# One transformer step with product-key experts: V rows gathered per token, one tile behind the u rows

## The chip, the cores and the metric

The kernel runs as one program on one core of a Trainium2 chip. The metric is the device time of one execution in microseconds (us); lower is better. Everything is float32.

## The reference

A layer computes adaLN modulation, an input projection, stick-breaking attention and a pooled branch, an output projection with residual, and then the part that matters here, PEER:

```
q  = h2 @ w_query                       # 8 heads, two halves of 128
s1, s2 = q[:,0] @ keys1, q[:,1] @ keys2 # 128 scores a half
v1,i1 = top16(s1); v2,i2 = top16(s2)
cand = v1[:,None] + v2[None,:]          # 256 sums
best, sel = top16(cand); idx = i1*128+i2 at sel
gate = softmax(best)
act  = gelu(h2 . u_tab[idx])            # one dot product an expert
out  = sum((gate*act) * v_tab[idx])     # 8*16 = 128 experts a token
x    = x + gate2 * RMSNorm(out)
```

There are 1024 prompt tokens (8 tiles of 128) and 64 sample tokens (one tile, called tile 0). `u_tab` and `v_tab` have 16,384 rows of 1024 floats (4 KB a row), so each token needs 128 rows of each.

## The kernel before, in words

`build` runs five stages one after the other: `modulation`, `projection`, `attention`, `output`, `experts`. The first four are left as they are but for the search of the sample tile, which runs inside `output` between its tiles.

`experts` (L1361) goes over tile 0 and then tiles 1 to 8; tiles 2 to 7 are a hardware loop. A tile has 8 heads, and a head is a unit of work of 16 slots (8 slots in tile 0, whose 128 partitions hold two experts of each of 64 tokens). A slot is one expert for each of 128 tokens:

- GpSimd (L1470 to L1500) issues, for each slot, an indirect DMA of 128 u rows of the next unit and one of 128 V rows of the current unit, 512 KB each. It is one queue in order: u, V, u, V. Each kind has a ring of 8 buffers, and an issue waits until the buffer's last reader is done. In all there are 1088 slots, so 2176 gathers.
- VectorE (L1601) multiplies each u buffer with the tile's h2 (held in PSUM) and sums the row: a *product*, one a slot. After 16 products it runs the whole *search* of one head of the next tile in one stretch (`Find.search`, L999), and then the unit's weights (gate times gelu).
- ScalarE (L1563) does the gelu, and turns each slot's 128 weights into a diagonal matrix (`diag`, L1580), four buffers.
- TensorE (L1685) computes `ps_y += diag.T @ vrow`, two matmuls of 512 columns a slot, which the profile shows as four records of weight load and matmul. Before each unit it computes one head's queries for the next tile (L942), with 128 columns, and in the middle of the unit that head's scores (L954).
- SyncE loads h2 and x1 and stores the tile.

So V of a unit is gathered while u of the next unit is, one unit behind it.

Of the kernel before, what the change touches and what calls it, by code (L numbers as in the profile page):

```python
# [11 lines left out]
P = 128  # L25
# [41 lines left out]
class Chain:  # L67
# [16 lines left out]
    def link_apart(self, ins, passed):  # L84

        self.add(ins)
        self.pass_apart(passed)

    def pass_apart(self, passed):  # L90
        self.wait()
        if not isinstance(self.base, int):
            self.eng.sem_inc(passed, 1)

def build(nc, A):
    with ExitStack() as outer:
# [6 lines left out]
        def sbuf(stack, name, shape, dt=F32):  # L104
# [8 lines left out]
            "h2_d": dram("h2_d", [TOK, D]),  # L113
            "const": sbuf(outer, "const", [P, C_END]),
# [4 lines left out]
        with ExitStack() as right:  # L119
# [10 lines left out]
            S["aux"] = sbuf(late, "aux", [P, 3 * D])  # L130
            S["w_out"] = right.enter_context(nc.sbuf_tensor("w_out_sb", [P, KC, D], F32, side="right"))
            for m, name in enumerate(("g1", "a2", "b2")):

                S[name] = [right.enter_context(nc.sbuf_tensor(name, [P, D], F32, side="right")),
                           S["aux"][:, m * D:(m + 1) * D]]
# [5 lines left out]
            S["w_q"] = sbuf(late, "w_q_sb", [P, KC, 2 * D])  # L141
            S["keys"] = sbuf(late, "keys_sb", [P, 2 * PH, NKEY])
            S["w_q_full"] = sem("w_q_full")
            S["find"] = Find(nc, S, late)
# [732 lines left out]
def is_sample(n):  # L877
    return isinstance(n, int) and n == 0

def width(n):

    return TOPK // 2 if is_sample(n) else TOPK

def slots(n, h):

    if is_sample(n):
        return width(0) * h
    return n * SLOTS + (TOPK * h - SLOTS // 2 if h >= 0 else -SLOTS // 2 - width(n - 1))  # L890

def known(n, h):

    return 2 * (h + 1) if is_sample(n) else n * PH + (PH + h + 1)

class Find:

    PASS = 28

    def __init__(self, nc, S, stack):
        sb = lambda n, s, d=F32: stack.enter_context(nc.sbuf_tensor(n, s, d))
        aux, const = S["aux"], S["const"]
        view = lambda c0, c1, **kw: aux[:, c0:c1].rearrange("p (a b) -> p a b", **kw)
        self.nc, self.w_q, self.keys = nc, S["w_q"], S["keys"]
        self.iota = const[:, C_IOTA:C_IOTA + TOPK]  # L910
        self.h2T = view(0, D, a=KC)
        self.onehot = view(D, D + 512, a=2 * TOPK)
        self.cand = view(D + 512, D + 768, a=TOPK)
        self.crep = view(D + 768, 2 * D, a=TOPK)
        self.srep = view(2 * D, 2 * D + 256, a=2)
        self.qTs = view(2 * D + 256, 2 * D + 512, a=2)
# [8 lines left out]
        self.idxf = sb("idxf", [P, TOPK])  # L925
        self.gexp = sb("gexp", [P, TOPK])
        self.gsum = sb("gsum", [P, 1])
        self.idx = sb("idx", [P, SLOTS], U32)
        self.gate = sb("gate", [P, SLOTS])
        self.idx0 = sb("idx0", [P, SLOTS // 2], U32)  # L930
        self.gate0 = sb("gate0", [P, SLOTS // 2])
        sem = S["sem"]
        (self.h2_tr, self.h2T_done, self.q_done, self.q_ready, self.s_done, self.s_read, self.gate_ask,
         self.gate_exp, self.idx_ready, self.v_used) = (
             sem(n) for n in ("h2_tr", "h2T_done", "q_done", "q_ready", "s_done", "s_read", "gate_ask", "gate_exp",
                              "idx_ready", "v_used"))

    def banks(self, ps_t, ps_q, ps_s):
        self.ps_t, self.ps_q, self.ps_s = ps_t, ps_q, ps_s

    def queries(self, pe, n, h):  # L942
        nc = self.nc
        if not (is_sample(n) and h == 0):

            pe.wait_ge(self.q_ready, n * PH + h)
# [7 lines left out]
    def scores(self, pe, n, h):  # L954
        nc = self.nc
        pe.wait_ge(self.q_ready, n * PH + (h + 1))
        if not (is_sample(n) and h < 2):

            pe.wait_ge(self.s_read, n * PH + (h - 1))
# [5 lines left out]

    def take_q(self, act, n, h):
        nc = self.nc
        act.wait_ge(self.q_done, n * PH + (h + 1))
        if not (is_sample(n) and h == 0):

            act.wait_ge(self.s_done, n * PH + h)
        nc.scalar.activation(self.qTs[:, :, :], self.ps_q[:, 0:2 * P].rearrange("p (k t) -> p k t", k=2), ACT.Copy)\  # L972
            .then_inc(self.q_ready, 1)

    def exp_gate(self, act, n, h):
        act.wait_ge(self.gate_ask, n * PH + (h + 1))
        self.nc.scalar.activation(self.gexp[:, :], self.gexp[:, :], ACT.Exp).then_inc(self.gate_exp, 1)  # L977

    def top16(self, own, passed, chains):  # L980

        nc = self.nc

        def step(ops):
            for op in ops[:-1]:
                own.add(op())
            own.link_apart(ops[-1](), passed)

        step([lambda v=v, src=src: nc.vector.max(v[:, 0:8], src) for v, src, _, _ in chains])  # L990
        for v, src, rep, index in chains:
            own.add(nc.vector.max_index(index[:, 0:8], v[:, 0:8], src))  # L992
            own.add(nc.vector.match_replace(rep, v[:, 0:8], src, LOWEST))  # L993
        own.pass_apart(passed)
        step([lambda v=v, rep=rep: nc.vector.max(v[:, 8:16], rep) for v, _, rep, _ in chains])
        step([lambda v=v, rep=rep, index=index: nc.vector.max_index(index[:, 8:16], v[:, 8:16], rep)  # L996
              for v, _, rep, index in chains])

    def search(self, own, dve, passed, n, h):  # L999

        nc = self.nc
        s = self.ps_s[h % 2]
        dve.wait_ge(self.s_done, n * PH + (h + 1))
        dve.sem_inc(passed, 1)
        self.top16(own, passed, [(self.v16[:, side, :], s[:, side * P:(side + 1) * P], self.srep[:, side, :],
                                  self.i16[:, side, :]) for side in range(2)])
        dve.sem_inc(self.s_read, 1)
        own.add(nc.vector.tensor_copy(self.i16f[:, :, :], self.i16[:, :, :]))
        own.link_apart(nc.vector.tensor_tensor(self.cand[:, :, :],
                                               self.v16[:, 0, :, None].broadcast_to([P, TOPK, TOPK]),  # L1010
                                               self.v16[:, 1, None, :].broadcast_to([P, TOPK, TOPK]), ALU.add),
                       passed)
        flat = self.cand[:, :, :].rearrange("p a b -> p (a b)")
        self.top16(own, passed, [(self.best[:, :], flat, self.crep[:, :, :].rearrange("p a b -> p (a b)"),
                                  self.sel[:, :])])

        nc.vector.tensor_scalar(self.gexp[:, :], self.best[:, :], self.best[:, 0:1], None, ALU.subtract)\  # L1017
            .then_inc(self.gate_ask, 1)

        own.add(nc.vector.tensor_scalar(self.selij[:, 0, :], self.sel[:, :], 4, None, ALU.logical_shift_right))  # L1020
        own.link(nc.vector.tensor_scalar(self.selij[:, 1, :], self.sel[:, :], TOPK - 1, None, ALU.bitwise_and))
        own.link(nc.vector.tensor_copy(self.selijf[:, :, :], self.selij[:, :, :]))
        own.link(nc.vector.tensor_tensor(
# [38 lines left out]
def output(nc, A, S):  # L1062
# [15 lines left out]
    with ExitStack() as st:  # L1078
# [52 lines left out]
        def _(act):  # L1131
# [50 lines left out]
            for t in range(NTILE - 1):  # L1182
# [13 lines left out]
                for h in heads.get(t + 1, [])[:1]:  # L1196
                    find.take_q(act, 0, h)
# [166 lines left out]

# [399 lines left out]
```

## Time and profile before

| what | value |
|---|---|
| median of 3 runs | 3820.19 us (3820.03 to 3820.32) |
| profiled execution, span from first to last instruction | 4199.6 us |
| experts stage in it, from the first u gather to the end | 904.6 to 4199.6 us |
| mean granted TensorE clock | 0.881 |
| busy: PE / PEld / DVE / ACT / POOL | 79% / 38% / 55% / 23% / 51% |
| moved by DMA | 1245.5 MB, of which 1141.0 MB on GpSimd's queue |

The profiled execution has no other time of its own than this span; it is 379 us longer than the median of the runs. PE is matmul, PEld weight load, DVE VectorE, ACT ScalarE, POOL GpSimd, SP SyncE. "Issue" as a releaser means that the profile shows nothing that was waited for; "remote" and "another core or an unknown queue" mean that it shows no one who ended the wait.

### The profile page before, as it was taken

The numbers are of one execution on the slowest core, as the hardware profiler recorded it, in microseconds if no ns is written. First come the engines' busy times: TensorE is split into PE (matmuls) and PEld (weight loads), VectorE is DVE, ScalarE is ACT, GpSimd is POOL, SyncE is SP. The second block draws the span as 40 slices with busy tenths as digits, with TensorE's granted clock in tenths as the row PEclk, the third lists the DMA queues.
The fourth block names the chain that finished last, engine by engine and source line by source line (L and its number), as shares of the span: only waits on it lengthen the run. The fifth ranks groups of instructions, "written<-read, shape, count | busy, mean of one in ns | idle before, by whom it ended". The sixth has DMA issues, their size and how long they took to land.

```text
span 4199.6 us, 38180 instructions
## 1 busy us (share of the span) xinstructions
PE 3314.8 (79%) x9348; PEld 1593.5 (38%) x9348; DVE 2313.6 (55%) x5821; ACT 950.0 (23%) x2161; POOL 2152.0 (51%) x2222
## 2 busy tenths in 40 slices
PE   8998989928777777877777777777777777887677
PEld 2454555513333333333333333333333333333222
DVE  2104552867755665555665655566555665556442
ACT  1003773312221221112112211211121121112111
POOL 0000300236566665666666666566666665666665
PEclk9999999969898898898888888888888888888888
DMA  9104102159999999999999999899999999999997
GB/s 357 64 15 126 32 19 113 61 188 352 344 357 359 353 359 354 347 368 343 341 359 347 350 356 344 332 354 355 360 347 358 358 357 348 343 363 358 361 362 303
DMA packets 365168, 1245.51 MB, mean 297 GB/s; under 512 B 52129, under 2 KB 57505, under 8 KB 362751
## 3 DMA queue, kind: packets, MB, share of 16 engines
q0 software_dynamic: 313504, 1141.02, 72.4%
q1 hardware_dynamic: 48852, 96.77, 6.6%
q10 hardware_dynamic: 2576, 5.10, 0.4%
q8 instruction: 85, 1.39, 0.1%
q14 instruction: 151, 1.23, 0.1%
HBM read 1220.34 MB, written 22.39 MB: 296 GB/s over the span
## 4 chain that ended last, share of the span: by engine, by line
PE 38%; issue 17%; another core or an unknown queue 9%; DVE 5%; DMA 4%; POOL 3%; ACT 1%; DVEq 0%; POOLq 0%; ACTq 0%; SPq 0%
PE ps_y L1692 33%; PE ps_q L950 5%; DMA urow<-in_u_tab,idx 3%; POOL urow L1473 2%; POOL vrow L1473 1%; DMA vrow<-in_v_tab,idx 1%; DVE urow L1612 1%; ACT diag L1580 1%; DVE aux L993 0%; PE ps_s L961 0%; DVE i L996 0%; DVE sel L996 0%; DVE i L992 0%; DVE aux L1029 0%
## 5 line engine op out<-in xcount | busy, mean ns | idle before, releaser
L1692 PE MATMUL ps_y<-vrow,diag 128*128 128x512 f32 (+1 forms) x4352 | 2220.8, 665 | 647.5 <-issue 329.9
L1612 DVE CUSTOM_DVE_ANT_0 urow<-urow,ps_h 128x1024 f32<-128x1024 f32 x1088 | 1299.8, 1220 | 1025.2 <-DMA urow<-in_u_tab,idx 865.6
L1692 PEld LDWEIGHTS ps_y<-vrow,diag 128*128 128x128 f32 (+1 forms) x4352 | 884.3, 209 | 1893.6 <-issue 1576.9
L1473 POOL DMA_INDIRECT vrow<-in_v_tab,idx x1088 | 1031.6, 948 | 785.7 <-issue 287.4
L1473 POOL DMA_INDIRECT urow<-in_u_tab,idx x1088 | 1030.7, 947 | 430.5 <-issue 282.8
L1580 ACT ACTIVATE diag<-const,wgt 128x128 f32<-128x128 f32 x1024 | 373.1, 396 | 1766.2 <-PE ps_y L1692 643.3
L950 PE MATMUL ps_q<-aux,w_q_sb 128*128 128x128 f32 x2048 | 271.7, 292 | 58.1 <-issue 49.4
L950 PEld LDWEIGHTS ps_q<-aux,w_q_sb 128*128 128x128 f32 x2048 | 263.9, 207 | 94.4 <-issue 93.2
L1293 POOL TENSOR_TENSOR xo<-xo,ot 128x1024 f32<-128x1024 f32 (+1 forms) x9 | 21.1, 2343 | 352.2 <-DVE ot L1249 352.2
L530 PE MATMUL ps_z<-hT,w_in_sb 128*128 128x512 f32 (+1 forms) x576 | 190.5, 491 | 4.6 <-DVE hT L448 4.6
L625 POOL MEMSET kTs<- 128x384 f32 x1 | 0.4, 418 | 322.7 <-POOLq L344 322.7
L530 PEld LDWEIGHTS ps_z<-hT,w_in_sb 128*128 128x128 f32 x576 | 95.1, 192 | 96.4 <-issue 90.3
L977 ACT ACTIVATE gexp<-gexp 128x16 f32<-128x16 f32 x72 | 15.5, 216 | 440.6 <-DVE gexp L1017 234.2
L824 DVE SCALAR_TENSOR_TENSOR spt<-ps_s,lt 128x512 f32<-128x512 f32 (+3 forms) x108 | 56.8, 526 | 97.8 <-ACT lt L780 89.6
L972 ACT ACTIVATE aux<-ps_q 128x256 f32<-128x256 f32 x64 | 24.3, 380 | 343.2 <-remote 323.5
L721 PE MATMUL ps_s<-spt,const 128*128 128x512 f32 (+3 forms) x216 | 86.6, 484 | 14.8 <-DVEq L846 14.6
L318 PE MATMUL ps_mod<-ada,silu 128*2 128x512 f32 x192 | 86.8, 608 | 14.0 <-DMA ada<-in_w_ada 14.0
L1612 DVE DVE_READ_ACCUMULATOR2_ANT dots<- 128x1 f32 x1088 | 90.0, 83 | 0.7 <-issue 0.7
L713 PE MATMUL ps_s<-qz,kT 128*128 128x512 f32 (+3 forms) x192 | 80.6, 510 | 11.7 <-DMA kTs<-kT_d 11.7
L1681 PE MATMUL ps_tr<-const,h2n 128*128 128x128 f32 x64 | 14.3, 364 | 94.6 <-DMA h2n<-h_d 52.6
L1534 ACT ACT_TABLE_LOAD x65 | 83.4, 1283 | 1.1
L744 PE MATMUL ps_o<-wt,vz 128*128 128x512 f32 (+3 forms) x192 | 78.2, 489 | 0.0
(181 smaller groups left out, 2341.3 us busy)
## 6 DMA issues: line engine op xcount, KB each, us to landing
ada<-in_w_ada SPq DMA_DIRECT2D x12, 2048.0 KB, 12.5
urow<-in_u_tab,idx POOLq DMA_INDIRECT x1088
vrow<-in_v_tab,idx POOLq DMA_INDIRECT x1088
w_in_sb<-in_w_in SPq DMA_DIRECT2D x8, 1024.0 KB, 17.9
w_q_sb<-in_w_query SPq DMA_DIRECT2D x8, 1024.0 KB, 14.3
x<-in_x_p ACTq DMA_DIRECT2D x8, 512.0 KB, 6.6
w_out_sb<-in_w_out SPq DMA_DIRECT2D x8, 512.0 KB, 7.0
xo<-in_x_p SPq DMA_DIRECT2D x8, 512.0 KB, 3.7
```

Of the source, the lines that this page charges most:

```text
L318: last = nc.tensor.matmul(psum[c % 2][0:2, :], silu[:, 2 * k:2 * k + 2], ada[c % ADA][:, k, :], start=(k == 0), stop=(k == KC - 1))
L530: last = nc.tensor.matmul(z[:, 0:n], w_in[:, k, w0:w0 + P], hT[:, k, c0:c0 + n], start=(k == 0), stop=(k == KC - 1))
L713: nc.tensor.matmul(z[:, u["c0"]:u["c1"]], lhsT, rhs, start=True, stop=True, skip_group_check=True).then_inc(z_done, 1)
L721: last = nc.tensor.matmul(z[:, c0:c1], ntri, spt[m % NS][:, c0:c1], start=False, stop=True, skip_group_check=True)
L744: last = nc.tensor.matmul(o[:, c0:c1], vz[b][:, u["h"], u["kb"], :], w[:, c0:c1], start=u["opens"], stop=u["closes"], skip_group_check=True)
L824: op = nc.vector.scalar_tensor_tensor(out=spt[m % NS][:, c], in0=ps_z[m % NZ][:, c], scalar=0.0, in1=lt[m % NS][:, c], op0=ALU.max, op1=AL ...
L950: last = nc.tensor.matmul(self.ps_q[:, side * P:(side + 1) * P], self.w_q[:, k, c * P:(c + 1) * P], self.h2T[:, k, :], start=(k == 0), sto ...
L1473: nc.gpsimd.indirect_dma_start(ring[k % RING][:, :], None, A[table][:, :], bass.IndirectOffsetOnAxis(ap=places[:, col:col + 1], axis=0)).t ...
L1534: nc.scalar.activation(gelu[h % 2][:, 0:w], dots[h % 2][:, 0:w], ACT.Gelu).then_inc(gelu_done, 1)
L1580: nc.scalar.activation(diag[s % DIAGS][:, :], ident, ACT.Copy, scale=weight)\
L1612: nc.vector.tensor_tensor_reduce(out=urow[k % RING][:, :], in0=urow[k % RING][:, :], in1=ps_h[:, :], scale=1.0, scalar=0.0, op0=ALU.mult, ...
L1692: last = nc.tensor.matmul(ps_y[0:rows, c], diag[s % DIAGS][:, 0:rows], vrow[k % RING][:, c], start=(s == 0), stop=(s == PH * width(n) - 1))
```

## The change

- **V by token.** A V gather takes the 128 experts of one token into 128 partitions, not one expert of 128 tokens. There are as many V gathers as before (64 for tile 0, 128 for each other tile). The indices of a tile are transposed on TensorE (`turn`, `take_idx`) for it, and so are its weights (`take_w`).
- **Weights in one column.** Token t = 32b + g is column g of a stationary of 32 columns that is zero elsewhere, and its result goes to the 32 output rows from 32b. `put_w` writes the weights of four tokens (b = 0 to 3) in one ScalarE instruction; the diagonals are gone.
- **A tile behind.** `DUE` says how many V items are due by each u slot: those of tile n from slot 8 of tile n+1 to its end. Tile 0 has u gathers alone, and all 128 V items of tile 8 come after the last u slot.
- **Search in 16 steps.** One step of the search of a head behind each product (two behind each in tile 0), six units ahead of use.
- **Queries and scores at once.** Those of all eight prompt tiles are computed in the first 16 units, 512 columns at a time, behind the transposes of all of h2; the scores go to DRAM (8.4 MB) and are read back head by head, 128 KB each.
- The rings have 6 u and 6 V buffers instead of 8 and 8; nothing is a loop any more; the gain of the last norm is loaded for every tile.

The core of the diff:

```
+LAG = 2
...
+    RU, RV, RW = 6, 6, 3
...
+    def tokens(n):
+        begin[n] = len(ITEMS)
+        quads = 4 if n else 2
+        ITEMS.extend((n, g, a) for g in range(32) for a in range(quads))
+        end[n] = len(ITEMS)
...
+    DUE = [(0, 0)] + [x for n in range(NT) for x in ((first(n + 1) + 8, begin[n]), (first(n + 2), end[n]))]
...
+        def target(q):
+
+            return q + PH - LAG if LAG <= q <= LAST - PH + LAG else None
...
         def _(sp):
...
+            for t in range(NT):
+                if t >= 2:
+                    sp.wait_ge(tr_done, 2 * (t - 1))
+                sp.dma_start(h2ld[t % 2], S["h2_d"][t * P:(t + 1) * P, :]).then_inc(h2ld_in[t % 2], 16)
...
+            for z in range(2 * PH):
+                r, h = divmod(z, PH)
+                sp.wait_ge(s_copied, 2 * (z + 1))
+                sp.dma_start(S["s_d"][4 * r:4 * r + 4, h].rearrange("t p c -> p t c"),
+                             sstage[z % 2].rearrange("p (t c) -> p t c", t=4)).then_inc(s_out[z % 2], 16)
...
         def _(pool):
...
+            for q, (n, h) in enumerate(UNITS):
+                pool.wait_ge(idx_ready, known(n, h))
+                for k in range(width(n)):
+                    s = slot(n, h, k)
+                    gather_u(s, n, width(n) * h + k)
+                    for v in items(s):
+                        gather_v(v)
+            for v in items(NU):
+                gather_v(v)
...
         def _(act):
...
+            def put_w(v):
...
+                W = (Wp if n else Ws)[m % RW]
+                src = wT[n % 2][:, 0:32 * quads].rearrange("p (a g) -> p a g", a=quads)[:, :, g]
+                nc.scalar.activation(W[:, :, 31], src, ACT.Copy).then_inc(W_ready, 1)
...
+                if q < 2 * PH:
+                    copy_q(q, 0)
+                    if q:
+                        copy_scores(q - 1)
+                    copy_q(q, 1)
+                elif q == 2 * PH:
+                    copy_scores(q - 1)
+                if 1 <= q <= LAST - PH + LAG - 1:
+                    load_scores(q - 1)
+                for k in range(width(n)):
+                    at_slot(slot(n, h, k))
+                    if k == width(n) * 3 // 4:
+                        ask_gate(q)
+                do_gelu(q)
...
         def _(dve):
...
+                    if k == 1 and q:
+                        weights(q - 1)
+                    if t is not None:
+                        tn, th = UNITS[t]
+                        j = t - PH
+                        if k == 0:
+                            dve.wait_ge(sc_full[j % 2], 16 * (j // 2 + 1))
+                        for i in ([k] if n else [2 * k, 2 * k + 1]):
+                            find.step(own, dve, tn, th, i, sc[j % 2],
+                                      find.picked[:, :, :])
...
         def _(pe):
...
+                for half in range(2):
+                    f = slice(512 * half, 512 * (half + 1))
+                    last = nc.tensor.matmul(sums(n)[r, f], W[:, b, 31 - a:63 - a], vrow[v % RV][:, f],
+                                            start=(a == 0), stop=(a == 31), skip_group_check=True)
                 last.then_inc(v_used, 1)
...
+            for q, (n, h) in enumerate(UNITS):
+                if q < 2 * PH:
+                    queries(q, 0)
+                    if q:
+                        scores(q - 1)
+                    queries(q, 1)
...
+                    for v in items(s):
+                        add_item(v)
+            turn(NT, "w")
+            for v in items(NU):
+                add_item(v)
```

## Rows read from the trace of the kernel before

**Rows 1.** The page's slices: DMA busy in tenths, GB/s, 40 equal slices.
```profile
DMA  9104102159999999999999999899999999999997
GB/s 357 64 15 126 32 19 113 61 188 352 344 357 359 353 359 354 347 368 343 341 359 347 350 356 344 332 354 355 360 347 358 358 357 348 343 363 358 361 362 303
```

**Rows 2.** Windows: stretch, length, busy (instructions) of PE PEld DVE ACT POOL, clock, DMA, GB/s.
```profile
904.00:950.00 46.00, 20.31 (x69) 11.76 (x70) 22.26 (x37) 7.07 (x18) 30.46 (x33) 0.63 1.00 370
1000.00:1100.00 100.00, 87.74 (x311) 39.30 (x310) 75.77 (x227) 24.31 (x54) 62.55 (x66) 0.93 0.94 345
1500.00:2000.00 500.00, 385.97 (x1032) 186.74 (x1031) 299.36 (x759) 101.43 (x231) 312.69 (x330) 0.86 0.94 352
3500.00:4000.00 500.00, 375.48 (x922) 170.67 (x921) 286.98 (x688) 92.77 (x220) 315.57 (x334) 0.85 0.94 354
4150.00:4200.00 50.00, 39.01 (x91) 16.84 (x89) 7.06 (x13) 11.35 (x26) 18.24 (x20) 0.94 0.63 237
```

**Rows 3.** Groups by line, POOL, experts stage: busy, mean ns | idle before, releasers.
```profile
L1473 POOL DMA_INDIRECT vrow<-in_v_tab,idx x1088 | 1031.6, 948 | 785.7 <-issue 287.4 <-remote 280.1 <-PE ps_y L1692 113.7
L1473 POOL DMA_INDIRECT urow<-in_u_tab,idx x1088 | 1030.7, 947 | 430.5 <-issue 282.8 <-DVE dots L1612 101.2 <-PE ps_y L1692 39.7
```

**Rows 4.** Timeline of POOL in a middle tile: start, length, instruction, [idle before <-releaser].
```profile
1361.21 0.94 POOL L1473 DMA_INDIRECT vrow<-in_v_tab,idx  x1 [0.30 <-issue]
1362.45 0.94 POOL L1473 DMA_INDIRECT urow<-in_u_tab,idx  x1 [0.30 <-issue]
1367.21 0.94 POOL L1473 DMA_INDIRECT vrow<-in_v_tab,idx  x1 [3.82 <-remote]
```

**Rows 5.** The page's chain that ended last: shares of the span by engine.
```profile
PE 38%; issue 17%; another core or an unknown queue 9%; DVE 5%; DMA 4%; POOL 3%; ACT 1%; DVEq 0%; POOLq 0%; ACTq 0%; SPq 0%
```

**Rows 6.** Timeline of VectorE in one unit: search's ends, then products.
```profile
1321.05 0.50 DVE L990 MAX8 v<-ps_s 128x8 f32<-128x128 f32 x2 [0.26 <-issue]
...
1330.62 0.26 DVE L1058 TENSOR_SCALAR gate<-gexp,gsum 128x16 f32<-128x16 f32 x1
...
1331.03 1.22 DVE L1612 CUSTOM_DVE_ANT_0 urow<-urow,ps_h 128x1024 f32<-128x1024 f32 x1
...
1332.17 1.22 DVE L1612 CUSTOM_DVE_ANT_0 urow<-urow,ps_h 128x1024 f32<-128x1024 f32 x1
...
1361.62 1.22 DVE L1612 CUSTOM_DVE_ANT_0 urow<-urow,ps_h 128x1024 f32<-128x1024 f32 x1 [1.33 <-DMA urow<-in_u_tab,idx]
...
1364.18 1.22 DVE L1612 CUSTOM_DVE_ANT_0 urow<-urow,ps_h 128x1024 f32<-128x1024 f32 x1 [1.33 <-DMA urow<-in_u_tab,idx]
```

**Rows 7.** Timeline of TensorE: one head's scores, four V slots, one head's queries.
```profile
945.46 0.71 PE L961 MATMUL ps_s<-keys_sb,aux 128*128 128x128 f32 x4
946.11 7.08 PE L1692 MATMUL ps_y<-vrow,diag 128*64 128x512 f32 x16
953.12 3.94 PE L950 MATMUL ps_q<-aux,w_q_sb 128*128 128x128 f32 x32
```

**Rows 8.** Timeline of all engines at the start of the experts stage.
```profile
903.85 1.15 SPq L1437 DMA_DIRECT2D h2n<-h_d  x2
904.62 1.09 POOL L1473 DMA_INDIRECT urow<-in_u_tab,idx  x1 [5.90 <-POOLq L1078]
...
908.53 1.12 ACT L1528 ACTIVATE ps_h<-h2n 128x512 f32<-128x512 f32 x2 [14.37 <-DMA h2n<-h_d]
909.66 1.28 ACT L1534 ACT_TABLE_LOAD   x1
...
929.37 0.21 ACT L1534 ACTIVATE gelu<-dots 128x8 f32<-128x8 f32 x1 [18.42 <-issue]
929.48 0.58 ACT L1517 ACTIVATE aux<-ps_tr 128x512 f32<-128x512 f32 x1
...
930.12 1.11 PE L1681 MATMUL ps_tr<-const,h2n 128*128 128x128 f32 x4 [7.08 <-issue]
```

**Rows 9.** DMA issues by line: count, KB each, us from issue to landing.
```profile
h_d<-h2o SPq DMA_DIRECT2D x8, 512.0 KB, 3.8
```

More of the change, by code:

```diff
@@ L82, in link @@
         self.wait()
[L84 to L93, printed above, removed]
 def build(nc, A):
@@ new lines, in normalise @@
+    def normalise(self, own, dve, n, h, i):
+        nc, gexp = self.nc, self.gexp[h % 2]
+        own.wait()
+        if i == 0:
+            dve.wait_ge(self.gate_exp, n * PH + (h + 1))
+            own.add(nc.vector.tensor_reduce(self.gsum[:, :], gexp[:, :], AX_X, ALU.add))
+        elif i == 1:
+            own.add(nc.vector.reciprocal(self.gsum[:, :], self.gsum[:, :]))
+        elif n == 0:
+            for m in range(2):
+                p, c = slice(DEC * m, DEC * (m + 1)), slice(width(0) * h, width(0) * (h + 1))
@@ new lines, in items, with t_event @@
+    def items(s):
+        return range(due(s - 1) if s else 0, due(s))
+    NORM = {first(n + 2) + 20: n for n in range(NT - 1)}
+    FINISH = {first(n + 2) + 24: n for n in range(NT - 1)}
+    STORE = {first(n + 2) + 27: n for n in range(NT - 1)}
+    GATE = {n + 2: n for n in range(NT - 1)}
+    H2_AFTER = {first(n + 2) + 29: n + 3 for n in range(NT - 2)}
+    def t_event(n, what):
+        return T_ORDER.index((n, what))
+    T_SLOT = {}
+    for n in range(NT + 1):
+        T_SLOT[first(n) + 40 if n else 2] = (n, "idx")
+        T_SLOT[first(n + 1) + 3] = (n, "w")
@@ L1542, in copy_sum, with clear, norm @@
+            def clear(W, quads):
+                if quads == 4:
+                    act.wait_ge(s_mm, 4 * PH)
+                for i in range(RW):
+                    own.add(nc.scalar.activation(W[i].rearrange("p a c -> p (a c)"), const[:, 0:63 * quads], ACT.Copy,
+                                                 scale=0.0))
+                own.wait()
+            def norm(n):
+                r = slice(0, nrows(n))
+                act.wait_ge(v_used, end[n])
+                if n:
                     act.wait_ge(y_done, n)
-                nc.scalar.activation(ysum[0:rows, :], ps_y[0:rows, :], ACT.Copy).then_inc(y_free, 1)
@@ new lines, in transposes, with queries @@
+                    last.then_inc(tr_done, 1)
+            def queries(z, side):
+                r, h = divmod(z, PH)
+                if z:
+                    pe.wait_ge(q_copied, 2 * z + side - 1)
+                c = 2 * h + side
+                for k in range(KC):
+                    last = nc.tensor.matmul(ps_y[1][:, HALF * side:HALF * (side + 1)], w_q[:, k, c * P:(c + 1) * P],
+                                            h2T[:, k, HALF * r:HALF * (r + 1)], start=(k == 0), stop=(k == KC - 1))
+                last.then_inc(q_mm, 1)
@@ new lines, in turn @@
+            def turn(n, what):
+                m = t_event(n, what)
+                if m:
+                    pe.wait_ge(t_copied, m)
+                if what == "idx":
+                    pe.wait_ge(idx_ready, known(n, PH - 1))
+                    c, srcs = HALF, [find.idxF[n % 2][:, :]]
+                else:
+                    pe.wait_ge(w_ready, unit[n, PH - 1] + 1)
+                    c, srcs = HALF + P, [wgt[n % 2][:, :]]
+                for i, src in enumerate(srcs):
+                    if n:
+                        last = nc.tensor.transpose(ps_g[:, c + P * i:c + P * (i + 1)], src, ident)
+                    else:
+                        for half in range(2):
+                            r = slice(DEC * half, DEC * (half + 1))
+                            last = nc.tensor.matmul(ps_g[r, c:c + DEC], src[r, 0:DEC], ident[r, r], start=True,
+                                                    stop=True, skip_group_check=True)
+                last.then_inc(t_mm, 1)
@@ L1714, in constants @@
+            turn(NT, "w")
+            for v in items(NU):
+                add_item(v)
 def constants():
```

774 lines of the change are left out of this document (420 added, 354 removed).

## The prediction

> **What bounds the kernel now.** I read the page's slices first. From the ninth slice to the last the DMA engines are busy nine tenths or more and move about 350 GB/s [rows 1]; before that, in the four stages that the change leaves alone, they mostly are not. So the experts stage, 904.6 us to the end, is what counts: 3295 us for 2176 gathers of 512 KB, 1.514 us a gather in the profiled execution. The table of stretches then shows that no compute engine is full there: in 500 us PE has 386, DVE 299, POOL 313 and ACT 101 us of work [rows 2], and DMA is busy 0.94.
>
> Next I looked at who paces the gathers. GpSimd takes 0.94 us for one and 0.30 us before the next, 1.24 us a gather when nothing holds it [rows 4]. When DMA is behind, a product waits for its u row and products come 2.56 us apart (1361.62 to 1364.18), while one u and one V gather land: 1.28 us a gather, 410 GB/s [rows 6]. These two paces are close, and the kernel runs near both. What it loses is in GpSimd's idle time: 785.7 + 430.5 = 1216 us [rows 3], of which 2176 x 0.30 = 653 us is the step between two gathers; the other 563 us are waits. About half of them end with no releaser shown ("remote", 280 us), like the 3.82 us at 1367.21 [rows 4]; the rest end with a V matmul or a product, so a ring was full.
>
> The profiled execution is 379 us longer than the median of the runs. In its chain 9% of the span, 378 us, is "another core or an unknown queue" [rows 5]. I take the unknown waits for something that the runs mostly lack, an assumption. The runs' pace is then (3820.2 - 904.6) / 2176 = 1.340 us a gather, if the first four stages take in the runs what they take in the profile: 5% over the 1.28 us. So the bulk is near its floor, and the number of gathers does not change. The question is what the change does at the two ends, where u and V no longer go side by side. I make the sum as a difference, stage by stage, at the runs' pace, and add it to the median.
>
> **The change part by part.**
>
> *Start.* All of h2 has to be loaded and transposed before the first queries. The first load takes 4.7 us until it is used (903.85 to 908.53) [rows 8]. A further load waits for the transposes of two tiles earlier: 3.8 us to land [rows 9] + 2 x 1.11 us of transposes [rows 8] + issue, 6.4 us for two tiles, 26 us for eight. So h2T stands at some 30 us. ScalarE does the 16 copies (0.58 us each) [rows 8] in front of everything else, the first gelu included. Products wait too, for the gains that SyncE loads behind the eight h2 loads; that costs nothing, since the gelu comes later anyway.
>
> *Queries.* One head of four tiles is 16 matmuls of 512 columns, 32 records of 7.08 / 16 = 0.44 us [rows 7]: 14.2 us; its scores 16 records of 0.18 us [rows 7]: 2.8 us; with the copies between them 18 us a unit. Sixteen of these come to 227 us of query time, where the 64 heads before took 64 x 3.94 = 252 us [rows 7]. So the work stays as it was, but it all stands in the first 16 units. First gelu: 30 + 14.2 + a copy 0.6 + table load and gelu 1.5 = 46 us; the second unit ends at 46 + 18 = 64 us.
>
> *Tile 0.* The other six units have 8 products and a whole search each. A product takes 1.14 us in a row (1331.03 to 1332.17), a search 9.9 us (1321.05 to 1330.88) [rows 6]. That makes 8 x 1.14 + 9.9 + 0.2 = 19.2 us, taken as 20 with the waits between steps; TensorE's 18 us lie beside it. Six units: 120 us. Tile 0 takes 184 us, in which only 64 gathers go (82 us of DMA at 1.28): DMA has over half of it idle, where before the same time was full [rows 2].
>
> *Tile 1.* 128 u and 64 V gathers. VectorE: 8 x (16 x 1.14 + 9.9 + 0.2) = 227 us. TensorE: 8 x (18 + 8 V items x 4 x 0.44) = 257 us. DMA: 192 x 1.28 = 246 us, + 7 MB of scores and tiles at 410 GB/s, 17 us, = 263 us. Three engines near one length hide one another badly, and ScalarE waits in order for the queries, for the stored scores (3.8 us to land) [rows 9] and only then writes V's weights: 270 us, at least 263, at most 300.
>
> Tiles 0 and 1 together: 454 us. Before, their 256 gathers' worth took 256 x 1.340 = 343 us. **+111 us.**
>
> *Tiles 2 to 8.* The first 8 slots have no V: 8 x (1.14 + 9.9 / 16) = 14.1 us on VectorE, and h2 is copied between two units behind a table load and a gelu, 1.28 + 0.21 + 1.12 = 2.6 us [rows 8]: 16.7 us for 8 gathers. The other 248 take 248 x 1.28 = 317.4 us. Scores, h2, gain, x1 and y are 3.1 MB on the same DMA engines, 7.6 us. Together 341.7 us against 343: 7 x -1.3 = **-9 us.** The diagonals that ScalarE no longer makes (before it had 101 us of work in 500) [rows 2] and the search in steps (VectorE had 299 in 500) are worth nothing here: the paces of GpSimd and DMA hide both. Rings of 6 hold 12 gathers, 15 us at 1.28; the longest stop of a reader that I can name is some 5 us, the h2 copy and the final norm's VectorE part. With that cover gone each microsecond of it would be DMA's loss. Both ends for these tiles: all of the ring waits that are not of the unknown kind go, 563 - 379 = 184 us, 152 us of them in seven tiles; or 8 us a tile more, if a boundary drains both rings.
>
> *Tail.* 128 V items with no u beside them, after gelu, transposes, copy and the first weights, some 5 us. DMA's pace gives 128 x 1.28 = 164 us; TensorE's, if an item is four records of 0.44 us one after the other [rows 7], 227 us. The rows show only matmuls that all write the same output rows; items that follow each other in the changed kernel write different ones. I take 180, nearer to DMA. 185 us against 128 x 1.340 = 171: **+14 us,** ends -2 and +61.
>
> *Nothing:* the search of tile 0 inside the output stage (same operations; two more of 0.2 us a head), the last norm, unrolled loops.
>
> Sum: 111 - 9 + 14 = +116 us. 3820 + 116 = **3936 us.** On the profiled execution's own 4199.6 us the sum depends on the unknown waits: if they stay, 1.514 us a gather makes the two first tiles 388 us before, and the end is near 4250 us; if V's new distance covers them, near 3940.
>
> **The rivals.**
>
> *The tail and tile 1 go serially* (slower still). TensorE needs 1.77 us an item in the tail, and in tile 1 its 32 us units stand behind ScalarE's waits. For it: half the columns make a record no shorter (64 columns: 0.44 us) [rows 7]. Against: other output rows. Tail +47, tile 1 +15: 3998 us.
>
> *V's waits were real, and they go* (faster). Before, V of a unit cannot be used until VectorE has ended the unit's products, the 9.9 us search and the weights; GpSimd issues in order, so a full V ring stops u as well. After, weights stand a tile ahead. For it: ring waits with PE or DVE as releaser [rows 3]. Against: a ring of 8 and 8 lasts 16 x 1.28 = 20 us, longer than search and weights, and the runs' 1.340 us leaves only 5%. Price: the seven tiles at GpSimd's 1.245 us, 256 x 1.245 = 319 us and no more, 7 x (319 - 343) = -168; opening +102, tail -4: 3750 us. It decides from where DMA lands a gather in less than 1.28 us, and tile boundaries cost nothing.
>
> *It cancels* (no change). The seven tiles gain 16 us each at 327 us, half of the above: about 3823 us.
>
> *The change doesn't reach its aim:* in tile 0 two steps stand behind each product, so the search still delays; this is in the sum.
>
> **How the numbers follow.** Forecast, an opening that costs some 110 us and a bulk as before: 0.44, own range 3880 to 3965. Serial tail: 0.25. Real V waits: 0.21. Cancelling: 0.10. A measurement of this kernel tells about 0.2% (8 us) from no change. Faster 0.22, within 0.2% 0.08, slower 0.70. The range goes from part of the faster case, 3785, past the serial one to 4010 us.
>
> **What would show it.** Right: a hole in DMA's busy share of some 180 us from the start of the stage, with DVE products of tile 0 in groups 20 us apart, then some 270 us of tile 1; middle tiles 256 gathers in 330 to 345 us; a tail with GpSimd issuing V alone. Wrong: tile 0 under 140 us, middle tiles at 320 us or less, or a tail over 220 us. The forecast also falls if the first four stages take much less in the runs than in the profile, since then the pace that I compare with is too fast.

## The result, and the profile after

The changed kernel takes 3915.5 us (median of 4 runs, 3913.5 to 3918.6), the kernel before 3820.3 beside it: ratio 1.0249, 95% interval 1.0234 to 1.0263. It is 95 us slower. The forecast was 3936 us, 20.5 us above that.

The page's slices of the changed kernel, DMA busy in tenths and GB/s:

```profile
DMA  9201402115899999999999999999999999999998
GB/s 355 90 21 42 127 21 79 70 64 206 274 384 398 386 406 409 409 397 409 409 391 409 409 408 395 409 409 393 409 409 409 393 409 409 393 410 409 410 379 330
```

Beside [rows 1] there are two things to see. The hole that stood ahead of the experts stage has grown into it: the tenth and eleventh slices move 206 and 274 GB/s, where before the stage ran full from its start. And behind it the bulk moves 409 GB/s where the profiled execution before had some 355. The next experiments show that this second difference lies in that one execution, not in the kernels.

The same stage by stretches: start and length, busy time (instructions) of PE, PEld, DVE, ACT and POOL, granted clock, DMA share, GB/s:

```profile
901.00:934.00 33.00, 15.43 (x64) 12.47 (x64) 1.66 (x2) 10.32 (x19) 5.79 (x6) 0.50 0.73 255
934.00:952.00 18.00, 17.31 (x38) 7.43 (x38) 5.49 (x12) 1.70 (x3) 4.67 (x5) 0.83 0.45 147
973.00:1081.80 108.80, 99.54 (x302) 50.30 (x300) 103.51 (x331) 32.58 (x51) 46.57 (x47) 0.98 0.82 262
1081.80:1349.60 267.80, 215.88 (x615) 81.03 (x616) 215.45 (x578) 48.58 (x99) 181.23 (x191) 0.93 1.01 390
3049.10:3389.20 340.10, 241.99 (x516) 46.69 (x514) 222.85 (x584) 32.04 (x71) 240.99 (x256) 0.97 1.02 404
3719.70:3906.00 186.30, 180.14 (x527) 46.73 (x525) 4.60 (x9) 9.89 (x39) 117.91 (x126) 1.00 0.97 370
```

These are the h2 transposes, the first queries, the last six units of tile 0, tile 1, one of the middle tiles, and the tail. Which resource is full changes from stretch to stretch: in tile 0 TensorE and VectorE together (99.5 and 103.5 of 108.8 us) with DMA at 262 GB/s; from tile 1 on DMA (390, then 404 GB/s); in the tail TensorE (180 of 186 us). In the profiled execution before, a stretch of the bulk had no such full resource [rows 2].

GpSimd's two groups (busy, mean ns | idle before, releasers) and the chain of waits by engine:

```profile
L1529 POOL DMA_INDIRECT vrow<-in_v_tab,idxT x1088 | 1025.5, 943 | 473.0 <-PE ps_y L1854 274.0 <-issue 192.4 <-DVE dots L1757 6.6
L1518 POOL DMA_INDIRECT urow<-in_u_tab,idx x1024 | 962.7, 940 | 370.7 <-issue 285.0 <-DVE dots L1757 85.7
```
```profile
DMA 33%; POOL 21%; PE 11%; issue 9%; DVE 3%; ACT 0%; SPq 0%; ACTq 0%; POOLq 0%; DVEq 0%
```

The 280 us of "remote" [rows 3] and the 9% of "another core or an unknown queue" [rows 5] have no counterpart. The chain is now DMA and the GpSimd that feeds it, where in that execution before it was TensorE with 38%.

**Where the 95 us are.** A landing is counted in the trace's packets of the gather queue, 128 to a gather. The kernel before has its price from the shortened kernel e1 below, whose profile is as fast as its runs: its own parts, and 340.7 us for each of the four tiles that it leaves out.

| part of the stage | forecast | measured: changed, before | difference |
|---|---|---|---|
| first issue to the 256th landing | +111 | 447.4 (901.3 to 1348.7), 348.9 (903.4 to 1252.3) | +98 |
| the next 1792 gathers | -9 | 2372.6 (to 3721.3), 1016.1 for three tiles (1252.3 to 2268.4) + 4 x 340.7 | -6 |
| the last 128 | +14 | 182.7 (to 3904.0), 167.1 (2268.4 to 2435.5) | +16 |
| last landing to the end | 0 | 12.8, 19.0 | -6 |
| start of the stage | 0 | 901.3, 903.4 | -2 |

The sum is +99 us. The profiled execution of the changed kernel, from which the column comes, took 3918.6 us, 98 us over the kernel before and 3 over the median of its runs.

### The profile page after: what moved, and what is told of

Its sections match the earlier page's. It is cut to its first block, busy times and chain, and to the rows that moved or that the text cites. A ratio compares the mean times of both kernels' runs of the same rounds, so it can differ in the third digit from the quotient of the medians.

```text
span 3916.8 us, 27996 instructions
## 1 busy us (share of the span) xinstructions
PE 3030.2 (77%) x7836; PEld 937.2 (24%) x7836; DVE 2239.9 (57%) x5829; ACT 620.8 (16%) x1368; POOL 2140.0 (55%) x2222
## 2 busy tenths in 40 slices
DMA packets 384492, 1267.75 MB, mean 324 GB/s; under 512 B 53606, under 2 KB 75366, under 8 KB 382154
## 4 chain that ended last, share of the span: by engine, by line
DMA 33%; POOL 21%; PE 11%; issue 9%; DVE 3%; ACT 0%; SPq 0%; ACTq 0%; POOLq 0%; DVEq 0%
DMA vrow<-in_v_tab,idxT 26%; POOL urow L1518 11%; POOL vrow L1529 10%; PE ps_y L1854 8%; DMA urow<-in_u_tab,idx 6%; PE ps_y L1800 2%; DVE urow L1757 2%; DMA s_d<-G 1%; DMA G<-h_d 1%; PE ps_g L1813 0%; PE ps_g L1790 0%; ACT G L1586 0%; DVE i L979 0%; DVE scratch L980 0%; DVE scratch L1016 0%
## 5 line engine op out<-in xcount | busy, mean ns | idle before, releaser
L1854 PE MATMUL ps_y<-vrow,keys_sb 128*32 128x512 f32 x4096 | 1855.3, 604 | 686.4 <-DMA vrow<-in_v_tab,idxT 685.7
L1757 DVE CUSTOM_DVE_ANT_0 urow<-urow,ps_h 128x1024 f32<-128x1024 f32 x1088 | 1326.4, 1220 | 904.8 <-DMA urow<-in_u_tab,idx 899.7
L1529 POOL DMA_INDIRECT vrow<-in_v_tab,idxT x1088 | 1025.5, 943 | 473.0 <-PE ps_y L1854 274.0
L1518 POOL DMA_INDIRECT urow<-in_u_tab,idx x1024 | 962.7, 940 | 370.7 <-issue 285.0
L1854 PEld LDWEIGHTS ps_y<-vrow,keys_sb 128*32 128x32 f32 x4096 | 368.9, 109 | 2162.0 <-issue 1026.5
L1800 PE MATMUL ps_y<-G 128*128 128x512 f32 x512 | 231.6, 609 | 0.7 <-ACT G L1680 0.7
L1636 ACT ACTIVATE keys_sb<-wT 128x4 f32<-128x4 f32 x256 | 48.1, 204 | 812.7 <-PE ps_y L1854 614.4
L1854 PE MATMUL ps_y<-vrow,G 128*32 128x512 f32 x256 | 95.0, 642 | 45.1 <-DMA vrow<-in_v_tab,idxT 41.9
L1800 PEld LDWEIGHTS ps_y<-G 128*128 128x128 f32 x512 | 98.5, 197 | 124.2 <-issue 123.1
L1518 POOL DMA_INDIRECT urow<-in_u_tab,idx_s x64 | 62.2, 972 | 110.2 <-DVE dots L1757 99.0
## 6 DMA issues: line engine op xcount, KB each, us to landing
vrow<-in_v_tab,idxT POOLq DMA_INDIRECT x1088, 12.1
urow<-in_u_tab,idx POOLq DMA_INDIRECT x1024, 12.1
G<-in_w_query SPq DMA_DIRECT2D x8, 1024.0 KB, 14.2
```

The source lines that it names most:

```text
L1518: nc.gpsimd.indirect_dma_start(urow[s % RU][:, :], None, A["u_tab"][:, :], bass.IndirectOffsetOnAxis(ap=places[:, col:col + 1], axis=0)).t ...
L1529: nc.gpsimd.indirect_dma_start(vrow[v % RV][:, :], None, A["v_tab"][:, :], bass.IndirectOffsetOnAxis(ap=idxT[n % 2][:, t:t + 1], axis=0)). ...
L1636: nc.scalar.activation(W[:, :, 31], src, ACT.Copy).then_inc(W_ready, 1)
L1757: nc.vector.tensor_tensor_reduce(out=urow[s % RU][:, :], in0=urow[s % RU][:, :], in1=ps_h[:, :], scale=1.0, scalar=0.0, op0=ALU.mult, op1= ...
L1800: last = nc.tensor.matmul(ps_y[1][:, HALF * side:HALF * (side + 1)], w_q[:, k, c * P:(c + 1) * P], h2T[:, k, HALF * r:HALF * (r + 1)], sta ...
L1854: last = nc.tensor.matmul(sums(n)[r, f], W[:, b, 31 - a:63 - a], vrow[v % RV][:, f], start=(a == 0), stop=(a == 31), skip_group_check=True)
```

## The experiments

**What a tile costs before (e1, e2).** All sums of the forecast stand on 1.340 us a gather, taken from the runs and not from the profiled execution.

```
-    run over NT = 8 prompt tiles in experts()        e1: NT = 4
-        experts(nc, A, S)                            e2: call removed
```

> The kernel before with the experts of four prompt tiles instead of eight; the other four tiles of the experts' output are left out. Four tiles of 256 gathers fewer, so the difference to 3820 us, divided by 4, is the real price of a middle tile before the change. Theory (the unknown waits of the profiled execution are absent from the runs, 1.340 us a gather): 4 x 343 = 1372 us fewer, 2448 us. Rival (the middle tiles cost in the runs what the profile shows, 385 us, and it is the first stages that are shorter): 4 x 385 = 1540 us fewer, 2280 us. A third possibility, that the middle tiles ran at the changed kernel's 340 us and the waits sat in the first tiles: 2460 us; it lies too near the theory to be told apart by this alone.

> The kernel before with the experts stage left out, so that only the four stages ahead of it run. Theory (these stages take in the runs what the profile shows): 905 us, within 10. Rival (the profiled execution's extra 379 us lie partly in these stages): clearly under 890 us, and at the extreme 526 us.

Measured: e1 2456.9 us (2453.3 to 2459.6), e2 905.3 us (903.2 to 908.1). Four tiles are 3819.7 - 2456.9 = 1362.8 us, 340.7 each, 1.331 us a gather. That lies between the theory (343) and the third possibility (340), nearer to the latter, and the first 256 gathers take more, 348.9 us in e1's trace. The four stages ahead take in the runs what they take in the profile. So the profiled execution's extra 379 us lay in the experts stage and in that execution alone; what made it slow is not shown. In e1's trace a middle tile of the code before looks like this:

```profile
1409.70:1750.30 340.60, 277.25 (x808) 138.46 (x808) 230.44 (x583) 79.39 (x178) 242.25 (x257) 0.91 1.01 399
```

DMA is nearly full (1.01, 399 GB/s), not at 0.94 and 352 as in [rows 2]. Read from the profiled execution alone, the kernel before seemed to have much room in every middle tile. It had little: e12 below takes it to 336.0 us and 405 GB/s.

**The opening (e3, e7).**

```
 e3: -LAG = 2            +LAG = 6        (search two units ahead, not six)
 e7: e3, and
-    queries of z = 0 to 15, one in each of the units 0 to 15, behind all h2 transposes
+    EARLY = {2: 0, 3: 1, 5: 2, 7: 3, 8: 4, 9: 5, 10: 6, 11: 7}
+    LATE = {8: 18, 9: 20, 10: 22, 11: 26, 12: 28, 13: 30, 14: 34, 15: 36}
+    (tiles 5 to 8 of h2 transposed in tile 1; gains first and scores on SyncE's queue)
```

> The changed kernel with the search two units ahead instead of six, and nothing else: tile 0 then holds two searches instead of six, but all its queries. Theory (in tile 0 TensorE's 18 us of queries a unit stand beside VectorE's 19 us, so taking one away uncovers the other): units of tile 0 stay between 16.5 and 18 us, 0 to 8 us less, 3907 to 3915 us. Rival (the search steps alone hold tile 0, the queries are hidden): units near 10 us in those four that lose their search, 32 us less, 3883 us.

> The changed kernel with the queries taken out of the opening: before tile 0 only tiles 1 to 4 of h2 are transposed, and they go beside tile 0's products; the first eight query units are spread over tiles 0 and 1 (units 2, 3, 5, 7 to 11) and the other eight over tiles 2 to 4, in halves, with the transposes of tiles 5 to 8 in tile 1; the search runs two units ahead instead of six, so that tile 0 holds two searches and not six; SyncE loads the scores; the gains are loaded first; the weights' blocks move out of the keys' buffer, which is needed longer. Theory (the opening's loss is the h2 transposes, the queries and the search that all stand in tile 0 before or beside its 64 gathers): tile 0 ends some 92 us after the stage begins instead of 180, tile 1 stays at DMA's 260 to 268, tiles 2 to 4 stay near 340: 88 us less, 3827 us. Rival 1 (the queries only move, since TensorE's 7 us pieces stop V and the rings run dry): tiles 2 to 4 lose 15 us each, 3870 us. Rival 2 (the opening waits for something else, the loads or GpSimd): over 3895 us.

Measured: e3 3908.9 us (ratio to before 1.0226, 1.0209 to 1.0243), 6.5 us less, as the theory said; its six units take 97.5 / 6 = 16.25 us, a little under the 16.5 to 18 expected. e7 3865.3 us (1.0113, 1.0096 to 1.0130), 50 us less, between the theory (3827) and its first rival (3870), and nearer to the rival. The late part of tile 0 in e3, then tile 0, tile 1 and tile 2 in e7, same columns as above:

```profile
973.00:1070.50 97.50, 93.08 (x281) 46.53 (x280) 64.31 (x165) 21.12 (x37) 40.33 (x43) 1.00 0.80 274
```
```profile
901.00:1019.60 118.60, 82.98 (x236) 43.75 (x236) 94.45 (x213) 22.90 (x42) 66.83 (x70) 0.81 0.96 356
1019.60:1281.00 261.40, 183.38 (x465) 56.11 (x465) 215.13 (x578) 43.22 (x91) 181.53 (x192) 0.91 1.02 401
1281.00:1624.80 343.80, 262.72 (x656) 65.81 (x654) 223.00 (x584) 39.38 (x87) 238.92 (x254) 0.97 1.02 399
```

In e3 VectorE falls by 39 us, from 103.5 of 108.8 to 64.3 of 97.5 us, and the stretch by only 11, because TensorE stays at 93.1 of 97.5. Only when the queries go too does DMA fill (356 GB/s over the whole of tile 0, where the changed kernel has 254). e7 moves the transposes, the queries and the gains together, so what each of them is worth is not told apart. Tiles 0 and 1 then end 380 us after the stage's start and not 448. Of the 88 us that I expected, the opening gave 68. Units 6 and 7 still held a whole search beside 8 products, 19.7 and 18.9 us each, and the first products waited while 3 MB of h2 came in beside the u rows. Some 18 us were then lost: tiles 2 to 4 took 343 to 345 us instead of 340, together 13 us (the 4.2 MB of scores that are stored there now are worth 10 us at 404 GB/s), and the last tile and the tail took 5 us more, for which no cause is shown. The rival that TensorE's pieces would drain the rings asked for 15 us a tile; these tiles lost some 4 each against 340, so the number lies near the rival's but not for its reason.

**The tail (e4, e5, e8).**

```
 e4: -  r = slice(32 * b, 32 * (b + 1))
     +  r = slice(32 * b, 32 * (b + 1)) if n < NT else slice(0, 32)     (start and stop to match)
 e5: -  for each item of tile 8: half 0, half 1
     +  for each two items u, u + 1: half 0 of u, of u + 1, half 1 of u, of u + 1
 e8: e5, and  row = (vrow + urow[2:])[w % 10]      (ten slots, not six)
```

> The changed kernel, where all items of the last tile add into output rows 0 to 31, so that the last tile's sums are not its own; instruction counts, gathers and waits are unchanged. Items that follow each other then write the same rows. Theory (in the tail the last records of an item overlap the first of the next because they write other rows; one after the other an item takes 4 x 0.44 = 1.76 us): the tail's 128 items go from 1.40 to 1.76 us, 46 us more, 3961 us, tail 232 us. Rival (the 1.40 us are DMA's landing and waits, and records of different rows do not overlap): no change, 3915 us.

> The changed kernel, where TensorE takes the last tile's items in pairs and alternates their matmuls (first half of one, first half of the other, then the second halves), so that each matmul follows one that writes other rows. Theory (records overlap when they write other rows, and TensorE at 1.40 us an item is what holds the tail over DMA's 1.28): an item falls below 1.28 us, the tail becomes DMA's 128 x 1.28 = 164 us and some 6 us of start and end, 170 us, 16 us less: 3900 us. Rival (the tail is DMA's already, or waiting for two rows costs what the order gains): 3915 us or a few more.

> The run with the paired tail, whose V rows now also go into the four u buffers that are idle then: ten slots instead of six. Theory (the paired tail lost because a pair holds two of six slots and waits for two rows, so that too few gathers are under way, and TensorE alone needs 134 us for the 128 items): tail at DMA's 1.28 us an item, 164 + 6 = 170 us instead of 216, 3903 us. Rival (something else in the paired order costs the time, as the weights' hand-over): 3949 us again.

Measured: e4 3954.3 us (1.0344, 1.0326 to 1.0361), 39 us more where 46 were expected (the changed kernel's own tail is 186 us, not 128 x 1.40 = 180); e5 3949.0 us (1.0320, 1.0296 to 1.0345), 33 us more where 16 less were expected; e8 3902.8 us (1.0214, 1.0197 to 1.0231), 13 us less than the changed kernel, and the expected time. The tails of e4, e5 and e8:

```profile
3715.00:3940.00 225.00, 224.01 (x526) 57.27 (x525) 4.46 (x9) 9.90 (x39) 117.99 (x126) 1.00 0.86 306
```
```profile
3721.00:3937.00 216.00, 138.94 (x527) 32.13 (x525) 4.39 (x9) 9.89 (x39) 118.00 (x126) 0.93 0.90 319
```
```profile
3713.30:3885.00 171.70, 125.07 (x519) 29.92 (x517) 4.60 (x9) 9.88 (x39) 117.97 (x126) 1.00 1.01 401
```

TensorE's busy time, the first column after the length, tells it. With all items in one quarter of the rows TensorE has 224 us of work, one item after the other; in the changed kernel's order 180; in pairs 139. So records that write other rows do overlap, and the more so the more often the rows change. But in e5 the time did not follow TensorE down. Its waits there, and GpSimd's:

```profile
L1870 PE MATMUL ps_y<-vrow,keys_sb 128*32 128x512 f32 x512 | 134.4, 654 | 76.5 <-DMA vrow<-in_v_tab,idxT 76.5
```
```profile
L1529 POOL DMA_INDIRECT vrow<-in_v_tab,idxT x126 | 118.0, 937 | 92.4 <-PE ps_y L1870 61.9 <-issue 26.1 <-PE ps_y L1854 4.4
```

TensorE waits 76.5 us for rows and GpSimd 62 us for TensorE: each for the other, which is a ring that is too short. A gather lands 12.1 us after its issue in the changed kernel (median of 1088), and a pair holds two of six slots until it has ended. The granted clock of this stretch is 0.93, so part of TensorE's 134 us went at the lower level. Ten slots end this: the granted clock is 1.00, DMA is full at 401 GB/s, and TensorE waits for rows after each pair of items, which takes it 1.91 us:

```profile
3791.41 1.91 PE L1882 MATMUL ps_y<-vrow,keys_sb 128*32 128x512 f32 x8 [0.66 <-DMA vrow<-in_v_tab,idxT]
```

Ten slots without the pairs were not run, so how the 13 us are shared between the two is open.

**Bytes in the middle tiles (e6, e9).**

```
 e6: +  for dst in (sc, sx): act.dma_start(dst[j % 2], S["s_d"][n - 1, h])     (loaded twice)
 e9: -  act.dma_start(h2n, S["g2_d"][0:1].broadcast_to([P, D]))  for every tile
     +  the same once, into gains
```

> The changed kernel, where every load of stored scores is issued a second time into spare space, and the search waits for both: 64 further loads of 131 KB, 8.4 MB. Theory (DMA sets the pace of tiles 1 to 8, busy share over 1.0 at 404 GB/s there): 8.4 MB / 404 GB/s = 21 us more, 3936 us, a middle tile 340.0 to 342.6 us. Rival (GpSimd's issue of 1.24 us a gather or ring waits set it, and DMA has room): no change, 3915 us.

> The changed kernel, where the gain of the prompt tiles is loaded once into space that is free after the start, instead of again for every tile: 6 loads of 0.52 MB fewer, and the next tile's h2 is loaded right after the one before is copied. Theory (DMA sets the pace): 3.1 MB / 404 GB/s = 7.8 us less, 3907 us. Rival (the pace is set elsewhere): 3915 us. If it gains much more than 8 us, the reload delayed something at the tile's boundary.

Measured: e6 3939.5 us (1.0308, 1.0291 to 1.0325), +24; e9 3908.3 us (1.0226, 1.0209 to 1.0243), -7. A middle tile of each:

```profile
3063.40:3406.60 343.20, 240.96 (x516) 46.48 (x514) 223.22 (x584) 31.98 (x71) 240.42 (x256) 0.98 1.02 404
```
```profile
3045.50:3384.30 338.80, 239.88 (x516) 46.29 (x514) 222.86 (x584) 32.16 (x71) 240.30 (x256) 0.98 1.02 404
```

340.1 us becomes 343.2 with 1.05 MB more and 338.8 with 0.52 MB fewer, at 404 GB/s in both. The bytes beside the gathers are paid in full (at 404 GB/s they are worth 2.6 and 1.3 us, an estimate; 3.1 and 1.3 were measured). That rules GpSimd's 1.24 us out as the pace of the middle tiles.

**What the code before lost between its tiles (e11, e12).** The change also makes V's weights a tile ahead, does the search in steps and writes the loops out. Two kernels try the second rival's mechanism, and the loops, in the code before.

```
 e11: ScalarE:  -  exp_gate(search of n + 1);  do_gelu(next unit)
                +  do_gelu(next unit);  exp_gate(search of n + 1)
      VectorE:  -  products;  search;  weights
                +  products;  search up to best[:, 0:16];  weights;  rest of the search
 e12: e11, and  -  with eng.Fori(0, NT - 2) as i:    +  for i in range(NT - 2):
```

> The kernel before with one thing moved: ScalarE's gelu goes ahead of the search's exponential, and VectorE makes the weights of V in the middle of the search, not behind it, so that V's matmuls can start some 7 us sooner in every unit. Nothing of the changed kernel's order is in it. Theory (V's wait for the search was covered by the rings, as the forecast took it): at most the 9 us by which a middle tile stands over DMA's 331 us can go, and I expect under 3 of them: 3800 to 3820 us. Rival (V's waits were real, and are what separates a middle tile from DMA's pace): 8 to 9 us a tile, 3745 to 3760 us.

> The version of the kernel before that makes V's weights in the middle of the search, with its loop over tiles 2 to 7 written out, so that no engine jumps back at a tile's end; the changed kernel has no loop either. In that version's trace VectorE stands 5.9 us at each turn of the loop with no releaser shown, and GpSimd then waits 8.8 us for a u slot. Theory (the jump costs this, and the rings don't hide it): six turns of 7 to 8.8 us, 42 to 53 us less than 3807, 3754 to 3765 us. Rival (the stand belongs to the change of tile, to the transposes and queries that come first in it): no change, 3807 us.

Measured: e11 3807.2 us (0.9962, 0.9948 to 0.9976), 14 us under the kernel before, where its rival asked for 60 to 75; e12 3789.8 us (0.9914, 0.9898 to 0.9931), another 17 us, where 42 to 53 were expected. Weights ahead of the search's end gain under 2 us a tile: V's waits were nearly all covered. The stand at the loop's turn in e11, VectorE and then GpSimd:

```profile
1796.34 1.22 DVE L1613 CUSTOM_DVE_ANT_0 urow<-urow,ps_h 128x1024 f32<-128x1024 f32 x1 [5.92 <-issue]
```
```profile
1798.38 0.94 POOL L1474 DMA_INDIRECT urow<-in_u_tab,idx  x1 [8.82 <-DVE dots L1613]
```

With the loop written out, in e12, VectorE has no idle gap over 4 us in the middle tiles, and GpSimd's longest wait at the same place is shorter:

```profile
1797.41 0.93 POOL L1474 DMA_INDIRECT vrow<-in_v_tab,idx  x1 [5.78 <-DVE dots L1613]
```

So the loop's turn did cost, 3.5 us each: 17 us over five turns, not six (tile 4: 339.7 to 336.0 us, e11 and then e12):

```profile
2087.90:2427.60 339.70, 281.88 (x808) 132.93 (x807) 230.41 (x582) 80.38 (x178) 241.79 (x257) 0.95 1.01 401
```
```profile
2082.90:2418.90 336.00, 279.35 (x812) 129.38 (x811) 231.06 (x583) 80.07 (x179) 242.20 (x256) 0.98 1.02 405
```

My expectation counted GpSimd's whole wait as the price, but most of it (5.78 of 8.82 us) stays: it is the search that stands between two groups of products. e12 is the fastest version here, 32 us under the kernel before and 126 under the changed one.

The Trainium skill, Advanced Engine Details and Errata, Control Flow Timing, gives about 51 ns for an unconditional branch. VectorE's stand of 5.9 us is over a hundred times that, so the branch alone does not explain it. One thing in e11's trace stands at the same place: in the 20 us around this turn (1780 to 1800) its two instruction queues move three packets each, in the 80 us before it one and four; e12 has none and one in the same 20 us. That VectorE waited for its instructions is a reading of this, not shown.

**The gains of the change's own line together (e10).** It joins e7, e8 and e9.

> The three versions that gained, together: the late queries, the paired tail with ten V slots, the gain loaded once. Theory (they act in different stretches, so they add up): 3865 - 12.6 - 7.1 = 3845 us. Rival (the late queries' own rest, 8 us in the tail and the last tile, was a waiting ring, and goes too): 3835 us. None of the theories has it under the kernel before.

Measured: 3847.1 us (1.0066, 1.0050 to 1.0083), as the theory added it up. The tail:

```profile
3660.60:3832.00 171.40, 125.01 (x519) 29.91 (x517) 4.61 (x9) 9.88 (x39) 118.01 (x126) 1.00 1.01 400
```

The changed order can be mended by 68 us and is then still 0.7% over the kernel before: 256 gathers take 379 us to land from its first issue, where before they took 349.

## Why the prediction was right, and where it was off

*Base.* Right. The unknown waits were absent from the runs, and a middle tile costs 340.7 us for my 343. But the first 256 gathers cost 349, because the code before has a start too; I gave it the pace of the bulk. That is 6 of the 13 us by which the opening was oversized.

*Start.* Near: h2T stood after 33.6 us (30 forecast). Products did wait for the gains, as the wait of 39.10 us shows. "That costs nothing, since the gelu comes later anyway" held for this wait, but another one stood behind it:

```profile
932.34 1.21 DVE L1746 TENSOR_TENSOR io<-io,G 2x1024 f32<-2x1024 f32 x1 [39.10 <-DMA io<-mod_d]
934.90 16.56 PE L1800 MATMUL ps_y<-G 128*128 128x512 f32 x32 [0.69 <-ACT G L1680]
951.77 0.23 DVE L1730 CAST idxT<-ps_g 128x64 uint32<-128x64 f32 x1 [12.51 <-PE ps_g L1836]
955.44 0.21 ACT L1602 ACTIVATE gelu<-dots 128x8 f32<-128x8 f32 x1 [2.05 <-DVE dots L1757]
```

Five products were done by 939.3 us. Then VectorE's copy of tile 0's transposed indices stands among the products, and TensorE makes that transpose behind both halves of the first queries. They took 16.6 and not 14.2 us: the granted clock of this stretch is 0.83, so part of it went at the lower of the two levels (1.2 of 2.4 GHz), and before it, when TensorE had only the transposes between loads, it was 0.50. So VectorE stood 12.5 us, and the first gelu came after 54 us, not 46. I had not named this copy.

*Tile 0.* The total is near (180.5 for 184) by luck, since two errors cancel: the first two units took 72 us, not 64, and the other six 17.9 each, not 20. My VectorE term of 19.2 was the mis-sized one: it was busy 103.5 us in the six units, 17.3 each. TensorE's term holds:

```profile
1011.32 13.90 PE L1800 MATMUL ps_y<-G 128*128 128x512 f32 x32
1025.05 1.05 PE L1813 MATMUL ps_g<-keys_sb,G 128*128 128x128 f32 x8
1028.19 1.52 PE L1813 MATMUL ps_g<-keys_sb,G 128*128 128x128 f32 x8 [2.08 <-ACT G L1586]
1029.51 12.69 PE L1800 MATMUL ps_y<-G 128*128 128x512 f32 x26
```

From 1011.32 to 1029.51 is a unit of queries, its scores and the next queries, 18.2 us for my 18. With two searches instead of six the units still take 16.25 us (e3), so this one alone holds them there.

*Tile 1.* 267.8 for 270, and set by DMA (1.01), which I had at 263. TensorE, which I had at 257, was busy 215.9 us.

*Tiles 2 to 8.* 340.0 for 341.7, on DMA's term: e6 and e9 move it by bytes alone. Of what I put at nothing, the written-out loops were worth some 3.5 us a turn in the code before (e12). The change spends that again on the scores that it carries through memory and the gain that it loads again: it moves 1267.75 MB in all, e12 with the same gathers 1245.07.

*Tail.* 186 us from the last product to the last V matmul, for 185. I took 180 "nearer to DMA" between 164 and 227. It is TensorE, at 1.40 us an item, and neither end; no row gave 180, so that the number fits is luck. In the changed kernel six items (24 records) take 8.54 us; in e4 four items (16 records) 7.03 us, 1.76 each:

```profile
3799.77 8.54 PE L1854 MATMUL ps_y<-vrow,keys_sb 128*32 128x512 f32 x24
```
```profile
3799.54 7.03 PE L1854 MATMUL ps_y<-vrow,keys_sb 128*32 128x512 f32 x16
```

*End.* I put the last norm at nothing, and that holds: from the last V matmul to the end are 10.6 us in e1 and 10.4 in the changed kernel. The 6 us of the table's row lie ahead of it. When the last V row has landed, TensorE has 8.4 us of matmuls left in e1 (2435.5 to 2443.9) and 2.4 in the changed kernel (3904.0 to 3906.4). In e1 and then in the changed kernel, ScalarE's first instruction behind the last matmul:

```profile
2443.94 1.02 ACT L1543 ACTIVATE ysum<-ps_y 128x1024 f32<-128x1024 f32 x1 [6.46 <-PE ps_y L1692]
```
```profile
3906.41 1.28 ACT L1653 ACT_TABLE_LOAD   x1 [15.84 <-PE ps_y L1854]
```

Counted to the last matmul, the tail costs 10 us more than before, not the 14 of the forecast.

*The rivals.* The serial tail is refuted by e4, which had to force it. "V's waits were real" asked for 319 us a middle tile; the changed kernel, whose weights stand a tile ahead, takes 340.0, and e11 gains 14 us from weights that stand a little earlier. "It cancels" fails with it, since it asked for 327.

So the forecast's mechanism was right (an opening that costs some 100 us and a bulk at DMA's pace), and its sum was 20.5 us above the median and 17 above the profiled execution (3918.6 us). Of these 17, 13 lie in the opening, 6 between the last landing and the end and 2 at the start, less 3 in the middle and 2 in the tail. These make 16; the last 1 us is not accounted for.

## What to carry to other kernels

Before you gain in a bulk, check that it isn't already at the pace of its transfers in the runs, not only in one profiled execution; a shorter copy of the kernel prices a tile by the difference. A reorder that separates two streams pays at both ends for what it frees in the middle, and work that is gathered "once, in front" is paid at the opening, where nothing stands beside it. When two engines are equally full in a stretch, taking work off one of them shows little (e3) until the other gives way too (e7).

## What was not expected of the hardware

- Matmuls of 32 output columns: 1.76 us an item of four records into the same rows, 1.40 when each item goes to other rows, and 0.95 when every matmul does (1.91 us a pair in e8, at a granted clock of 1.00; e5's 134.4 us for 128 items are 1.05, at 0.93).
- A ring's depth against the landing time sets the rate when the reader takes rows in pairs: 319 GB/s with six slots, 401 with ten, while the DMA share read 0.90 and 1.01 (the granted clock differed too, 0.93 and 1.00). The share alone would have called the first nearly full.
- VectorE stood 5.9 to 6.0 us at each of five turns of a loop whose body was a whole tile (5.92 in the one shown).
